# A two-block fp32 transformer kernel on one core: a rearranged hand-over between its stages, vector units moved within the down projections, keys before queries

## The chip, the core and the metric

The kernel runs on one core of a Trainium2 chip. The metric is the device time of one launch in microseconds, here the median of three runs. In all that follows PE is TensorE, DVE is VectorE, ACT is ScalarE, SP is the engine that issues nearly all DMAs, and an order of instructions is fixed for each engine by hand: the engines run ahead of one another as far as semaphores let them.

## What is computed

The reference takes x (256 tokens by 1024 features) through eight residual stages, all in fp32. Cut to what matters here:

```
x  = x + ga1 * mlstm(modulate(x))                      # stage "lstm"
x  = x + ga2 * conv_glu(modulate(x));  x = rmsnorm(x)  # stage "f0", then the final norm of block one
for each of the six sublayers f1, gla, f2, f3, mla, f4:
    h = rmsnorm(x, g_pre) * (1 + scale) + shift
    x = x + w * gate * rmsnorm(fn(h), g_post)          # fn: swiglu, gla_mixer, swiglu, swiglu, mla_mixer, swiglu
```

The shifts, scales and gates of the second block are products of silu(c) with conditioning matrices. swiglu is (silu(h Wg) * (h Wu)) Wd with a hidden width of 2816. mla_mixer makes a key and value latent of 256 from the output of f2, a query latent of 384 from its own input, normalises both, and multiplies them by key, value and query matrices.

## The kernel before, in words

**Products in three parts.** Each fp32 operand is split into a rounded part (type fp32r) and the rest. A product is three matmuls: rounded by rounded, rounded by rest, rest by rounded. The weights come as 219 chunks of 1 MB (`raw`), 128 x 2048 each. ACT rounds a chunk (`act_split`, line 223) and DVE takes the rest (`dve_split`, line 230). A raw slot is free again when the chunk five before it has been used (`s_pe`), so SP's issue of a chunk waits for PE.

**Vector units.** The conditioning product is done on DVE in 192 units of 0.5 MB: `dve_mod_unit` (line 675) multiplies 128 rows of 1024 weights with silu(c) and sums them. Two buffers (`mring`) hold the next two. SP issues a unit's transfer only behind the chunk that stands for it and only when the unit two before is done. The lists `UP_UNITS` and `DOWN_UNITS` say how many units DVE does after each split of a swiglu. `dve_ffn` does the split of down chunk d + 2, then `DOWN_UNITS[f][d]` units.

**The end of a stage.** A down or output projection of 8 or 22 feature tiles adds into four PSUM banks, one for each token tile t (of 128 tokens) and half h (of 512 columns). All chunks but the last run over all four banks. The last one or two run bank by bank (`pe_out_last`), so that bank (0,0) is complete first: with one chunk a bank takes 6 matmuls, with two it takes 12. Two chunks are used by f0 to f4, one by lstm, gla and mla.

**The seam.** `dve_boundary` and `act_boundary` then work for each token tile: ACT squares both halves of the rows of the output (line 493) and sums them, makes the mean of the first half plus epsilon (line 501, `uu`), and a logarithm and an exponential give the row's factor (lines 505, 506). DVE multiplies the output by the gate row (`dve_product`, line 597) and adds it to X (`dve_update`, line 606 or 610); ACT takes the norm of the new X the same way; DVE scales the rows (`dve_pre`, line 558, `XN`, two halves); PE transposes eight tiles (`pe_pre`, line 480); ACT applies shift and scale to each (`act_scaled`, line 545, one bank of four tiles at a time for t = 0); DVE rounds four tiles and takes the rest (`dve_pre_split`, lines 568 and 570), or one by one for t = 1 (lines 576, 580). After f0 a second norm of X (the final one of block one, line 617) stands between update and next norm. lstm and f0 have no norm of their output (`PLAIN`).

**The next stage's start.** Its first product (`pe_ffn`, `pe_gla`) takes all eight feature tiles of token tile 0. Before the last of them PE does the eight transposes of token tile 1, then goes through token tile 1. In f1 to f4 the transposes of token tile 0 stand before the last three matmuls of the stage before; behind lstm, f0, gla and mla they stand behind the last matmul.

**The latents.** `pe_kv` runs the key and value latent's two chunks with the transposes of token tile 1 between them, then the query latent: chunk DQ (4 half banks' worth) and, when chunk DQ_UQ has its rest, the last third of it; then the keys from the kv latent, the query latent's sum of squares, and the values.

## Time and profile before

| | us |
|---|---|
| median of 3 runs (1504.69 to 1509.45) | 1506.56 |
| the profiled execution's own time | 1504.5 |
| its span, first to last instruction | 1502.7 |
| PE busy | 1396.1 (93%) |
| DVE busy | 1132.1 (75%) |
| ACT busy | 800.9 (53%) |
| granted TensorE clock, mean | 0.973 |

Read it so: the span and the run's own time differ by 1.8 us that lie around the instructions. PE is busy for 1396.1 of 1502.7 us, so it is idle for 106.6; its busy time holds stretches in which the granted clock was 0.5 instead of 1.0. In the timeline a row merges like instructions of an engine: start, duration, engine, line, operation, and in brackets the idle time before and what ended it.

### The profile page before, as it was taken

How to read it: one execution, taken by the hardware profiler on the slowest of the kernel's cores; microseconds unless marked ns; L12 is line 12 of the kernel's file. 1: busy time of each engine (PE TensorE's matmuls, PEld its weight loads, DVE VectorE, ACT ScalarE, POOL GpSimd, SP SyncE). 2: the span in 40 equal slices, each digit the busy share in tenths (PEclk: the TensorE clock that was granted, in tenths of full speed). 3: DMA queues.
4: the chain of work that ended last, by engine and by line, in shares of the span. 5: the costliest groups of instructions: out<-in, count | busy, mean ns of one | idle time of the engine just before them, and what ended most of it. 6: DMA issues, size and time to landing. Idle time of an engine off the chain costs nothing.

```text
span 1502.7 us, 19113 instructions
## 1 busy us (share of the span) xinstructions
PE 1396.1 (93%) x7530; PEld 1195.5 (80%) x7530; DVE 1132.1 (75%) x1559; ACT 800.9 (53%) x1170; POOL 1.4 (0%) x6
## 2 busy tenths in 40 slices
PE   5989987899998999989989999989999896899997
PEld 4978876788876888878968888868887785688886
DVE  6787696699875988678677988679997764587653
ACT  6613534666636655365466555386554643665542
POOL 0000000000000000000000000000000000000000
PEclk9999998999999999999999999999999999999999
DMA  9576313477783887856544888849988530465551
GB/s 384 204 259 233 122 67 126 164 267 262 259 336 113 320 305 285 299 208 246 200 154 163 316 292 297 304 159 337 325 311 319 176 140 1 140 255 211 184 191 56
DMA packets 62713, 337.78 MB, mean 225 GB/s; under 512 B 6928, under 2 KB 9360, under 8 KB 34208
## 3 DMA queue, kind: packets, MB, share of 16 engines
q1 hardware_dynamic: 62160, 335.35, 61.6%
q8 instruction: 60, 0.98, 0.3%
q0 software_dynamic: 288, 1.05, 0.2%
q14 instruction: 29, 0.24, 0.1%
q10 hardware_dynamic: 176, 0.16, 0.0%
HBM read 335.49 MB, written 1.05 MB: 224 GB/s over the span
## 4 chain that ended last, share of the span: by engine, by line
PE 65%; DVE 17%; DMA 8%; ACT 7%; issue 3%; SPq 0%; ACTq 0%; DVEq 0%
PE bank L234 63%; DVE wlo L230 6%; DMA mring<-m_stream 6%; DVE mring L675 2%; DMA raw<-w_stream 2%; ACT T L545 1%; ACT whi L223 1%; ACT rstd L493 1%; ACT SGC L845 1%; DVE GU L885 1%; DVE T L907 1%; DVE rd L1338 1%; PE bank L480 1%; DVE SGC L896 1%; DVE SGC L893 1%
## 5 line engine op out<-in xcount | busy, mean ns | idle before, releaser
L234 PE MATMUL bank<-hh,whi 128*128 128x512 f32 (+1 forms) x2192 | 674.3, 368 | 16.0 <-DVE wlo L230 15.5
L230 DVE TENSOR_TENSOR wlo<-raw,whi 128x2048 fp32r<-128x2048 f32 x219 | 500.1, 2287 | 68.6 <-ACT whi L223 68.4
L234 PE MATMUL bank<-hh,wlo 128*128 128x256 f32 x1896 | 532.1, 281 | 0.0
L223 ACT ACTIVATE whi<-raw 128x2048 fp32r<-128x2048 f32 x219 | 418.0, 1913 | 160.7 <-PE bank L234 84.1
L234 PEld LDWEIGHTS bank<-hh,whi 128*128 128x128 f32 x2192 | 395.1, 190 | 93.9 <-DVE wlo L230 17.2
L234 PEld LDWEIGHTS bank<-hh,wlo 128*128 128x128 f32 x1896 | 360.2, 190 | 0.0
L675 DVE SCALAR_TENSOR_TENSOR mring<-mring,con 128x1024 f32<-128x1024 f32 x160 | 195.0, 1220 | 52.4 <-DMA mring<-m_stream 52.1
L234 PE MATMUL bank<-whi,hid_hi 128*128 128x512 f32 x440 | 173.7, 395 | 3.6 <-DVE wlo L230 3.6
L234 PE MATMUL bank<-whi,hh 128*128 128x512 f32 x480 | 163.1, 411 | 13.9 <-DVE hh L570 13.3
L234 PE MATMUL bank<-whi,hid_lo 128*128 128x512 f32 x440 | 172.6, 392 | 0.0
L234 PE MATMUL bank<-wlo,hid_hi 128*128 128x512 f32 x440 | 172.5, 392 | 0.0
L234 PEld LDWEIGHTS bank<-whi,hh 128*128 128x128 f32 x480 | 94.7, 197 | 39.9 <-issue 14.6
L837 ACT ACTIVATE GU<-bank 128x512 f32<-128x512 f32 x100 | 59.2, 592 | 100.6 <-PE bank L234 100.5
L234 PEld LDWEIGHTS bank<-whi,hid_hi 128*128 128x128 f32 x440 | 83.3, 189 | 21.4 <-DVE wlo L230 4.4
L234 PEld LDWEIGHTS bank<-whi,hid_lo 128*128 128x128 f32 x440 | 83.3, 189 | 17.7
L234 PE MATMUL bank<-wlo,hh 128*128 128x512 f32 x240 | 97.1, 405 | 0.0
L234 PEld LDWEIGHTS bank<-wlo,hid_hi 128*128 128x128 f32 x440 | 83.2, 189 | 16.8
L885 DVE TENSOR_TENSOR GU<-GU,bank 128x512 f32<-128x512 f32 x100 | 68.4, 684 | 33.4 <-ACT GU L837 33.3
L849 ACT ACTIVATE hid_hi<-T 128x256 fp32r<-128x256 f32 x110 | 46.0, 418 | 82.9 <-DVE T L907 82.9
L545 ACT ACTIVATE T<-bank,mod,coef 128x128 f32<-128x128 f32 x128 | 47.1, 475 | 26.8 <-PE bank L480 26.8
L907 DVE TENSOR_TENSOR T<-SGC,GU 128x256 f32<-128x256 f32 x100 | 42.3, 423 | 17.1 <-ACT SGC L845 15.0
L234 PEld LDWEIGHTS bank<-wlo,hh 128*128 128x128 f32 x240 | 47.4, 198 | 9.3
(290 smaller groups left out, 1267.1 us busy)
## 6 DMA issues: line engine op xcount, KB each, us to landing
raw<-w_stream SPq DMA_DIRECT2D x219, 1024.0 KB, 5.4
mring<-m_stream SPq DMA_DIRECT2D x192, 512.0 KB, 5.0
con<-const_d SPq DMA_DIRECT2D x1, 1472.0 KB, 10.8
XF<-xT SPq DMA_DIRECT2D x1, 1024.0 KB, 13.2
XC<-ctxT SPq DMA_DIRECT2D x1, 1024.0 KB, 12.5
y<-OUT SPq DMA_DIRECT2D x4, 256.0 KB, 2.9
cb<-c_row POOLq DMA_DIRECT2D x1, 512.0 KB, 7.4
con<-c_row POOLq DMA_DIRECT2D x1, 512.0 KB, 4.0
```

The lines of the kernel that those rows point to most:

```text
L223: nc.scalar.activation(w_hi(c, 0, CW), raw[:, c % RAW_SLOTS], ACT.Copy).then_inc(s_hi, 1)
L230: nc.vector.tensor_tensor(w_lo(c, 0, CW), raw[:, c % RAW_SLOTS], w_hi(c, 0, CW).bitcast(f32), ALU.subtract).then_inc(s_lo, 1)
L234: return nc.tensor.matmul(out, lhsT, rhs, start=start, stop=True, skip_group_check=True)
L480: nc.tensor.transpose(turned(t, j), XN[:, j * P:(j + 1) * P], ident).then_inc(s_tpn, 1)
L493: ins = nc.scalar.activation(junk, src(h), ACT.Square, accum_out=ss[:, n, h:h + 1])
L545: ins = nc.scalar.activation(TX[:, j], turned(t, j), ACT.Identity, bias=mod[:, m0 + j:m0 + j + 1], scale=coef[:, q, j:j + 1])
L675: nc.vector.scalar_tensor_tensor(out=mring[:, u % 2], in0=mring[:, u % 2], scalar=1.0, in1=(cb if u < COND_UNITS else cb2)[:], op0=ALU.mul ...
L837: nc.scalar.activation(GU[:, t % 2], banks[:, b:b + 2, SEQ:], ACT.Copy).then_inc(s_part, 1)
L845: nc.scalar.activation(SG[:, t % 3], gate, ACT.Silu).then_inc(s_silu, 1)
L849: nc.scalar.activation(hid_hi[:, t], T[:, t % 3], ACT.Copy).then_inc(s_hidhi, 1)
L885: nc.vector.tensor_tensor(GU[:, t % 2], GU[:, t % 2], banks[:, b:b + 2, 0:SEQ], ALU.add)\
L907: nc.vector.tensor_tensor(T[:, t % 3], SG[:, t % 3], value, ALU.mult).then_inc(s_prod, 1)
```

## The change

1. **Half means on DVE.** Line 501 leaves ACT (28 instructions); the new `dve_half` makes `uu` on DVE (28 instructions, each behind a new semaphore from ACT's first square), and ACT waits for it before the logarithm.
2. **First token tile in three pieces.** Of token tile 0, tiles 0, 1, 4, 5 go to bank 6 and are scaled on ACT, tiles 2, 3, 6, 7 go to bank 7 and are scaled on DVE (`dve_scaled`). DVE rounds them as tiles 0-1, 2-3 and 4-7, all three ahead of the update of token tile 1, and PE waits for a piece. The transposes come as two halves, and the second waits until tiles 0 to 3 have been scaled. The product of bank (1,0) moves ahead of `XN` of token tile 0, and ACT's square of it waits for that product.
3. **Units.** The units of a down projection are the same in number (14, and 12 in each of f1 to f3), but the last three splits have none before or between them but those of d = 7, and the coefficients are made one chunk sooner.
4. **Two chunks by token tile.** mla's last two chunks run bank by bank, as f0 to f4 do. lstm's and gla's run as chunk 2 for banks (0,0), (0,1), (1,0), chunk 3 for the same, then both for (1,1).
5. **Transposes** of token tile 0: half of them before the last three matmuls in f1, f2, f3 and now mla, the other half behind.
6. **Keys ahead of queries.** In `pe_kv` the keys come before the last third of the query latent, whose sum of squares moves into the values; DVE splits VALUES and DQ_UQ before the rotary key, and copies the keys before it builds `KRM`.

```diff
+        TAIL = [(i, n) for i in range(4) for n in range(2)]
+        HEAD_TAIL = [(0, 0), (1, 0), (2, 0), (0, 1), (1, 1), (2, 1), (3, 0), (3, 1)]
+        def pe_out_last(pe, c0, k0, hi, lo, order=TAIL, first=lambda: None, second=lambda: None, mid=None):
+            for i, n in order:
...
+                for g in range(2):
+                    if (i, n, g) == (3, 1, 1) and mid is not None:
+                        mid()
...
         def turned(t, j):
-            b, n = (j // 2, j % 2) if t else (6 + j // 4, j % 4)
+            b, n = (j // 2, j % 2) if t else (6 + j // 2 % 2, j // 4 * 2 + j % 2)
...
+        def pe_pre(pe, pre, t, halves=(0, 1)):
+            for half in halves:
+                pe.wait_ge(s_xn, 4 * PRES.index(pre) + 2 * t + half + 1)
+                for j in range(4 * half, 4 * half + 4):
+                    if t == 0 and j == 4:
+                        pe.wait_ge(s_t, MODULATED[pre] + 1)
+                    if t == 0 and j == 6:
+                        pe.wait_ge(s_vt, 2 * PRES.index(pre) + 1)
+                    nc.tensor.transpose(turned(t, j), XN[:, j * P:(j + 1) * P], ident).then_inc(s_tpn, 1)
...
+        def dve_half(dve, n):
+            if n in OTHERS:
+                dve.wait_ge(s_xsq, OTHERS.index(n) + 1)
+            else:
+                _, stage, t = ROW_NORMS[n]
+                dve.wait_ge(s_ysq, 4 * POSTS.index(stage) + 2 * t + 1)
+            nc.vector.tensor_scalar(uu[:, n:n + 1], ss[:, n, 0:1], 1.0 / D, EPS, ALU.mult, ALU.add).then_inc(s_uu, 1)
...
+        def dve_scaled(dve, name, tiles):
+            m0, _, q = PRE[name]
+            dve.wait_ge(s_tpn, turned_from(name) + bank_turned(0, tiles[-1]))
+            for j in tiles:
+                ins = nc.vector.tensor_scalar(TX[:, j], turned(0, j), coef[:, q, j:j + 1], mod[:, m0 + j:m0 + j + 1],
+                                              ALU.mult, ALU.add)
+            ins.then_inc(s_vt, 1)
...
         def dve_boundary(dve, stage):
             for t in range(2):
-                dve_product(dve, stage, t, 0)
...
+                if t == 0:
+                    dve_product(dve, stage, 0, 0)
+                elif pre:
+                    dve_scaled(dve, pre, (2, 3))
+                if stage not in PLAIN:
+                    dve_half(dve, rn("post", stage, t))
+                if t and pre:
+                    dve_first_piece(dve, pre, 0)
+                    dve_first_piece(dve, pre, 1)
+                dve_product(dve, stage, t, 1)
+                if t and pre:
+                    dve_scaled(dve, pre, (6, 7))
+                    dve_first_piece(dve, pre, 2)
                 dve_update(dve, stage, t)
                 if pre:
+                    dve_half(dve, rn("pre", pre, t))
+                if t == 0:
+                    dve_product(dve, stage, 1, 0)
...
-        DOWN_UNITS = [[2, 2, 1, 1, 2, 1, 2, 2, 1, 0, 0]] + [[1, 1, 1, 1, 1, 2, 1, 2, 2, 0, 0]] * 3 + [[0] * 11]
+        DOWN_UNITS = [[2, 2, 2, 2, 2, 2, 1, 1, 0, 0, 0]] + [[2, 1, 2, 1, 2, 1, 2, 1, 0, 0, 0]] * 3 + [[0] * 11]
...
-            after = {FT // 2 - 1: coefs}
+            after = {FT // 2 - 2: coefs}
...
             pe_pair(pe, DQ, 2)
-            pe.wait_ge(s_lo, DQ_UQ + 1)
-            for k in range(DT):
-                ins = mm3(bank[3][:, 0:SEQ], DQ_UQ, k, hhi[:, k], hlo[:, k], k == 0)
-            ins.then_inc(s_q2, 1)
+            pe.wait_ge(s_lo, KEYS + 1)
             pe.wait_ge(s_l, 2)
...
             ins.then_inc(s_pe, 1)
-            pe_stat(pe, N_QL)
+            pe.wait_ge(s_lo, DQ_UQ + 1)
+            for k in range(DT):
+                ins = mm3(bank[3][:, 0:SEQ], DQ_UQ, k, hhi[:, k], hlo[:, k], k == 0)
+            ins.then_inc(s_q2, 1)
             for n, (t, half, b) in enumerate(VALUE_BANKS):
+                if n == 2:
+                    pe_stat(pe, N_QL)
...
```

How the change moves DVE's instructions shows at three places. The first is the end of f1's down projection and the first half of the seam to gla. Line 675 (738 after) is a vector unit, 230 a weight split, 597 (653) the gate product, 610 (666) the update, 558 (613) the scaled rows. Before:

```order
L675 SCALAR_TENSOR_TENSOR mring,mod<-mring,con 128x1024 x2
L230 TENSOR_TENSOR wlo<-raw,whi 128x2048
L675 SCALAR_TENSOR_TENSOR mring,mod<-mring,con 128x1024 x2
L230 TENSOR_TENSOR wlo<-raw,whi 128x2048 x2
L687 TENSOR_TENSOR mod<-mod,cols 128x24
L691 SCALAR_TENSOR_TENSOR coef<-mod,cols 128x8
L597 TENSOR_TENSOR SGC<-bank,con 128x512 x2
L610 SCALAR_TENSOR_TENSOR X<-SGC,rr,X 128x512 x2
L558 TENSOR_SCALAR XN<-X,rr 128x512 x2
```

After:

```order
L738 SCALAR_TENSOR_TENSOR mring,mod<-mring,con 128x1024
L230 TENSOR_TENSOR wlo<-raw,whi 128x2048 x2
L750 TENSOR_TENSOR mod<-mod,cols 128x24
L754 SCALAR_TENSOR_TENSOR coef<-mod,cols 128x8
L230 TENSOR_TENSOR wlo<-raw,whi 128x2048
L653 TENSOR_TENSOR SGC<-bank,con 128x512
L518 TENSOR_SCALAR uu<-ss 128x1
L653 TENSOR_TENSOR SGC<-bank,con 128x512
L666 SCALAR_TENSOR_TENSOR X<-SGC,rr,X 128x512 x2
L518 TENSOR_SCALAR uu<-ss 128x1
L653 TENSOR_TENSOR SGC<-bank,con 128x512
L613 TENSOR_SCALAR XN<-X,rr 128x512 x2
```

No unit stands among the last three splits, and a third product stands before the scaled rows.

The second place is the same engine and seam from there to the scaled rows of token tile 1. Before:

```order
L597 TENSOR_TENSOR SGC<-bank,con 128x512
L568 CAST hh<-T 128x4x128
L570 TENSOR_TENSOR hh<-T,hh 128x4x128
L597 TENSOR_TENSOR SGC<-bank,con 128x512
L610 SCALAR_TENSOR_TENSOR X<-SGC,rr,X 128x512 x2
L568 CAST hh<-T 128x4x128
L570 TENSOR_TENSOR hh<-T,hh 128x4x128
L558 TENSOR_SCALAR XN<-X,rr 128x512 x2
```

After (588 is the new scaling of two tiles, 601 and 603 the rounding and the rest):

```order
L588 TENSOR_SCALAR T<-bank,coef,mod 128x128 x2
L518 TENSOR_SCALAR uu<-ss 128x1
L601 CAST hh<-T 128x2x128
L603 TENSOR_TENSOR hh<-T,hh 128x2x128
L601 CAST hh<-T 128x2x128
L603 TENSOR_TENSOR hh<-T,hh 128x2x128
L653 TENSOR_TENSOR SGC<-bank,con 128x512
L588 TENSOR_SCALAR T<-bank,coef,mod 128x128 x2
L601 CAST hh<-T 128x4x128
L603 TENSOR_TENSOR hh<-T,hh 128x4x128
L666 SCALAR_TENSOR_TENSOR X<-SGC,rr,X 128x512 x2
```

All of token tile 0 is now split before the update of token tile 1 begins.

The third place is DVE in the latents of mla, from the split of KEYS on (704, 767: a gate coefficient; 1798 to 1800, 1858 to 1860: the rotary key). Before:

```order
L704 SCALAR_TENSOR_TENSOR coef<-mod,cols 128x8
L1798 TENSOR_TENSOR KR<-bank,rd 128x256
L1799 TENSOR_TENSOR SGC<-bank,rd 128x256
L1800 TENSOR_TENSOR KR<-KR,SGC 128x256
L1798 TENSOR_TENSOR KR<-bank,rd 128x256
L1799 TENSOR_TENSOR SGC<-bank,rd 128x256
L1800 TENSOR_TENSOR KR<-KR,SGC 128x256
L230 TENSOR_TENSOR wlo<-raw,whi 128x2048 x2
L1900 MEMSET KRM 128x2048
```

After:

```order
L767 SCALAR_TENSOR_TENSOR coef<-mod,cols 128x8
L230 TENSOR_TENSOR wlo<-raw,whi 128x2048 x2
L1858 TENSOR_TENSOR KR<-bank,rd 128x256
L1859 TENSOR_TENSOR SGC<-bank,rd 128x256
L1860 TENSOR_TENSOR KR<-KR,SGC 128x256
```

The splits of VALUES and DQ_UQ stand in front of the rotary key.

## Rows read from the trace of the kernel before

**Rows 1.** Stretch in f1's down projection: length, busy us (PE, PEld, DVE, ACT, POOL), PEclk, DMA share, GB/s.

```profile
610.00:615.44 5.44, 5.44 (x26) 4.51 (x25) 2.85 (x3) 1.92 (x2) 0.00 (x0) 1.00 0.78 289
```

**Rows 2.** Timeline of PE: the transposes of token tile 0 at the seven seams.

```profile
252.35 1.10 PE L480 MATMUL bank<-con,XN 128*128 128x128 f32 x8 [1.66 <-DVE XN L558]
...
458.61 1.09 PE L480 MATMUL bank<-con,XN 128*128 128x128 f32 x8 [2.12 <-DVE XN L558]
...
654.94 1.09 PE L480 MATMUL bank<-con,XN 128*128 128x128 f32 x8 [2.85 <-DVE XN L558]
...
784.62 1.09 PE L480 MATMUL bank<-con,XN 128*128 128x128 f32 x8 [2.49 <-DVE XN L558]
...
980.57 1.97 PE L480 MATMUL bank<-con,XN 128*128 128x128 f32 x8 [3.05 <-DVE XN L558]
...
1175.05 1.96 PE L480 MATMUL bank<-con,XN 128*128 128x128 f32 x8 [3.01 <-DVE XN L558]
...
1300.55 1.21 PE L480 MATMUL bank<-con,XN 128*128 128x128 f32 x8 [2.50 <-DVE XN L558]
```

**Rows 3.** Timeline of PE: the transposes of token tile 1 at the same seams.

```profile
262.42 1.04 PE L480 MATMUL bank<-con,XN 128*128 128x128 f32 x8
...
469.80 1.03 PE L480 MATMUL bank<-con,XN 128*128 128x128 f32 x8
...
665.56 1.04 PE L480 MATMUL bank<-con,XN 128*128 128x128 f32 x8
...
795.23 1.03 PE L480 MATMUL bank<-con,XN 128*128 128x128 f32 x8
...
989.94 1.04 PE L480 MATMUL bank<-con,XN 128*128 128x128 f32 x8
...
1184.04 1.04 PE L480 MATMUL bank<-con,XN 128*128 128x128 f32 x8
...
1310.92 1.03 PE L480 MATMUL bank<-con,XN 128*128 128x128 f32 x8
```

**Rows 4.** Timeline of DVE at the seam from f1 to gla.

```profile
645.20 4.49 DVE L230 TENSOR_TENSOR wlo<-raw,whi 128x2048 fp32r<-128x2048 f32 x2
...
651.23 1.40 DVE L610 SCALAR_TENSOR_TENSOR X<-SGC,rr,X 128x512 f32<-128x512 f32 x2
654.40 0.88 DVE L558 TENSOR_SCALAR XN<-X,rr 128x512 f32<-128x512 f32 x2 [1.77 <-ACT rr L506]
```

**Rows 5.** Timeline of ACT at the same seam.

```profile
648.47 0.20 ACT L506 ACTIVATE rr<-rl 128x1 f32<-128x1 f32 x1
...
652.76 0.29 ACT L501 ACTIVATE uu<-ss,eps 128x1 f32<-128x1 f32 x1
...
655.72 1.50 ACT L545 ACTIVATE T<-bank,mod,coef 128x128 f32<-128x128 f32 x4 [0.45 <-PE bank L480]
```

**Rows 6.** Groups of DVE, shapes apart: times, then busy us and mean ns.

```profile
L570 DVE TENSOR_TENSOR hh<-T,hh 128x512 fp32r<-128x512 f32 x14 | 9.7, 692 | 0.5
...
L580 DVE TENSOR_TENSOR hh<-T,hh 128x128 fp32r<-128x128 f32 x56 | 15.4, 285 | 0.0
```

**Rows 7.** Three more stretches: behind a seam, in mla's latents, in f0's down projection.

```profile
656.30:663.10 6.80, 5.26 (x13) 3.61 (x12) 4.95 (x9) 5.58 (x18) 0.00 (x0) 0.50 0.45 154
1203.60:1209.20 5.60, 5.60 (x26) 5.60 (x27) 3.44 (x5) 0.08 (x1) 0.00 (x0) 0.50 0.00 0
418.00:424.00 6.00, 6.00 (x29) 4.95 (x28) 2.97 (x4) 3.59 (x2) 0.00 (x0) 1.00 1.00 388
```

**Rows 8.** Timeline of PE and of DVE in mla's latents.

```profile
1199.05 4.49 DVE L230 TENSOR_TENSOR wlo<-raw,whi 128x2048 fp32r<-128x2048 f32 x2
...
1203.59 0.80 PE L234 MATMUL bank<-hh,whi 128*128 128x256 f32 x2 [5.91 <-DVE wlo L230]
```

**Rows 9.** f0's down projection: PE before the last two chunks; the units' transfers.

```profile
443.71 0.50 PE L234 MATMUL bank<-whi,hid_hi 128*128 128x512 f32 x1 [2.57 <-DVE wlo L230]
...
DMA to landing us min/median/max: 3.5/5.4/7.0
```

More of the change, by code:

```diff
@@ L320, in pe_out_chunk @@
             ins.then_inc(s_pe, 1)
-        def pe_out_last(pe, chunks, k0, hi, lo, mid=None):
-            for i, (t, h) in enumerate(GROUPS):
-                for n, c in enumerate(chunks):
-                    for g in range(2):
-                        if i == 3 and n and g and mid is not None:
-                            mid()
-                        k = k0 + 2 * n + g
-                        ins = mm3w(out_bank(t, h), c, g * D + h * 512, tok(hi, k, t), tok(lo, k, t), False)
-                    if i == 3:
-                        ins.then_inc(s_pe, 1)
-                if i < 3:
+        TAIL = [(i, n) for i in range(4) for n in range(2)]
+        HEAD_TAIL = [(0, 0), (1, 0), (2, 0), (0, 1), (1, 1), (2, 1), (3, 0), (3, 1)]
+        def pe_out_last(pe, c0, k0, hi, lo, order=TAIL, first=lambda: None, second=lambda: None, mid=None):
+            for i, n in order:
+                t, h = GROUPS[i]
+                if (i, n) == (0, 0):
+                    first()
+                if (i, n) == (0, 1):
+                    second()
+                for g in range(2):
+                    if (i, n, g) == (3, 1, 1) and mid is not None:
+                        mid()
+                    k = k0 + 2 * n + g
+                    ins = mm3w(out_bank(t, h), c0 + n, g * D + h * 512, tok(hi, k, t), tok(lo, k, t), False)
+                if i == 3:
+                    ins.then_inc(s_pe, 1)
+                elif n:
                     ins.then_inc(s_yb, 1)
@@ L497, in act_row_rstd @@
                     act.wait_ge(s_ysq, ysq[0])
-                else:
-                    alink(act, ins)
-                if h == 0:
-                    alink(act, nc.scalar.activation(uu[:, n:n + 1], ss[:, n, 0:1], ACT.Identity, bias=eps[:, 0:1],
-                                                    scale=1.0 / D))
-                    if between is not None:
-                        between()
+                elif h:
+                    alink(act, ins)
+                else:
+                    ins.then_inc(s_xsq, 1)
+                    act.wait_ge(s_xsq, OTHERS.index(n) + 1)
+                if h == 0 and between is not None:
+                    between()
+            act.wait_ge(s_uu, n + 1)
             alink(act, nc.scalar.activation(rl[:, n:n + 1], ss[:, n, 1:2], ACT.Ln, bias=uu[:, n:n + 1], scale=1.0 / D))
@@ L525, in act_boundary @@
                     if t == 0 and stage in PLAIN:
-                        for b in range(2):
-                            act_scaled(act, pre, 0, b)
+                        act_scaled(act, pre, 0, (0, 1))
+                        act_scaled(act, pre, 0, (4, 5))
                 else:
@@ L532, in act_boundary, with act_scaled @@
             if pre:
-                act_scaled(act, pre, 1, None)
+                act_scaled(act, pre, 1, range(DT))
         def four(x):
             return x.rearrange("p (a b) -> p a b", a=4)
-        def act_scaled(act, name, t, b):
+        def act_scaled(act, name, t, tiles):
             m0, _, q = PRE[name]
             p0 = turned_from("f3" if name == "kv" else name)
-            act.wait_ge(s_h, U[name] + 2 * t)
-            for j in range(DT) if b is None else range(4 * b, 4 * b + 4):
+            act.wait_ge(s_h, U[name] + (2 if name == "kv" else len(PIECES)) * t)
+            for j in tiles:
                 act.wait_ge(s_tpn, p0 + bank_turned(t, j))
@@ L613, in dve_update @@
                 n = rn("fin", stage, t)
+                dve_half(dve, n)
                 dve.wait_ge(s_rr, n + 1)
@@ L1572, in pe_gla @@
             pe_gate_row(pe, "gla", (4, 5))
-            for j in range(2, 4):
-                out_chunk(j)
+            pe_out_last(pe, c + 15, 4, hhi, hlo, HEAD_TAIL, lambda: out_chunk(2), lambda: out_chunk(3))
             pe_pre(pe, "f2", 0)
@@ L1894, in dve_kv @@
             dve_gate_coef(dve, "mla")
+            dve_split(dve, VALUES)
+            dve_split(dve, DQ_UQ)
             dve.wait_ge(s_cs, 1)
@@ L1897, in dve_kv @@
             dve_rope(dve, KR[:, 0], KR[:, 1], *halves(5), s_kr)
-            dve_split(dve, VALUES)
-            dve_split(dve, DQ_UQ)
+            dve.wait_ge(s_pe, KEYS + 1)
+            for b in (0, 2):
+                nc.vector.tensor_copy(flat(KN[:, 2 * b:2 * b + 2]), bank[KEY_BANKS[b]][:]).then_inc(s_kn, 1)
             link(dve, nc.vector.memset(KRM[:], 0.0))
@@ L1904, in dve_kv @@
             ins.then_inc(s_kr, 1)
-            dve.wait_ge(s_pe, KEYS + 1)
-            for b in (0, 2):
-                nc.vector.tensor_copy(flat(KN[:, 2 * b:2 * b + 2]), bank[KEY_BANKS[b]][:]).then_inc(s_kn, 1)
             dve_latent(dve, 2, 3, N_QL, "g_q", (*halves(2), halves(3)[0]), qhi, qlo)
```

154 lines of the change are left out of this document (77 added, 77 removed).

## The prediction

> **What bounds the kernel now.** The page gives PE 93% of the span, so I looked for the rest in PE's idle time. Inside a stage there is none: in 5.44 us of a down projection PE is busy for all 5.44 (26 matmuls touch the stretch, 24 begin in it, one each 0.227) [rows 1]. The timeline has it at the seams: the transposes of token tile 0 wait for the scaled rows `XN`, 1.66 to 3.05 us at each of seven seams [rows 2]. I call P the start of the transposes of token tile 0 and P1 that of token tile 1. P1 is what a seam ends with: behind it PE always finds its next operands after about the same time, as everything there (scaling on ACT, rounding on DVE, the next weight split) hangs on these transposes. So a seam's gain is the shift of P1. From P to P1 it now takes 10.07, 11.19, 10.62, 10.61, 9.37, 8.99 and 10.37 us [rows 2, 3], for lstm to f0, f0 to f1, f1 to gla, gla to f2, f2 to f3, f3 to mla, and mla to f4. I call them A to G. In much of each such stretch TensorE runs at half rate: from 656.3 to 663.1 the granted clock is 0.50, the 1.2 GHz level [rows 7]. At E and F it has already fallen when the transposes come, which take 1.97 and 1.96 us there and 1.09 elsewhere, behind waits of 3.05 and 3.01 [rows 2].
>
> **Part one, P.** Take C. The product of bank (0,1) can follow at once when ACT has squared that bank, and the row's factor is there at 648.47 + 0.20 = 648.67 [rows 5]. But DVE is busy with two weight splits from 645.20 to 649.69 [rows 4], since it had done two vector units just before. Its update starts at 651.23. With no unit there, the splits are done as their chunks are rounded, and the update starts at about 648.8: 2.4 earlier. The mean `uu` stood on ACT between two squares, 0.29 [rows 5], 0.33 with its gap; DVE makes it while ACT squares the second half, so 0.33 goes once per norm of X. P moves by 2.7 at C. At E and F the same sum, from the same order of instructions, gives 2.9 each; at both the wait before P leaves about 0.1. At B the splits do not bind, since lstm and f0 need no norm of the output; two norms of X give 0.7. At A and D bank (0,1) is complete one bank's turn of 6 matmuls (6 x 0.227 = 1.36) sooner before the end of PE's work; with 0.33 that is 1.7, of which A can use 1.45 (its wait is 1.66 and 0.2 stays). At G it is complete two turns sooner: 2.7 + 0.33 = 3.1, which also the move of half the transposes ahead of three matmuls allows. Sum over A to G: 1.45 + 0.7 + 2.7 + 1.7 + 2.9 + 2.9 + 3.1 = 15.4 us. The product of bank (1,0), moved ahead of `XN`, costs 0.69 like row L570 [rows 6], and lies in the 1.77 that DVE waits for ACT before `XN` [rows 4]; without that cover it would cost up to 0.69 at each seam, 4.8 in all.
>
> **Part two, P to P1.** The new order fills DVE. From P: two tiles are transposed after 0.5; ACT scales two in 0.8 (four take 1.50 [rows 5]); DVE rounds tiles 0-1 and 2-3 in 0.75 each (a rest takes 0.285 for one tile and 0.692 for four [rows 6]; I take 0.42 for two, and 0.33 for the rounding); the product takes 0.6, the scaling of tiles 6-7 0.5, the third piece 1.1. The update can start at P + 5.0. From its start to `XN` it is 654.40 - 651.23 = 3.17 [rows 4], less 0.33, and 0.54 more to the transposes (654.94 - 654.40 [rows 2, 4]). So P1 = P + 8.4, whatever PE does: PE, which starts its matmuls at about P + 2.25, reaches the transposes at P + 7.4 and waits 1.0. At B a second norm and its product lie on that path, another 2.8: P1 = P + 11.2, and PE waits about 4 us there. The new scaling from PSUM on DVE has no row; for one tile it lies between the 0.285 of L580 and, if it were as slow as ACT, 0.47; I take 0.25 with overlap, the upper end adds 0.9 per seam. The differences to the present P1 - P are 1.7, 0, 2.2, 2.2, 1.0, 0.6, 2.0: 9.7 us.
>
> **The clock.** TensorE at half rate matters only where PE binds, which is behind P1. At B the new wait of 4 us ends there. Rows show the clock at 0.5 behind waits of 3.0 and 3.05 [rows 2], and a stretch of it lasts 5 to 7 us at C and in the latents [rows 7]; I take one of half that length, which costs 1.5. At the other six, waits come in pieces of at most 1.0 and I take 0.4 each, the part of such a loss that the wait before P1 does not absorb. Together -3.9.
>
> The Trainium skill, "TensorE: Matmul & The Clock Gate", part 1, says that idle time lets the chip gate TensorE to half rate, and that it needs sustained matmuls to come back; part 4 adds that transposes do not count as such. By that rule the wait at B, followed by transposes, is sure to cost what I charge, and the six others could pay the same. The trace agrees in that each seam's half-rate stretch takes in its transposes or what follows them.
>
> **Latents.** PE waits 5.91 us for DQ_UQ's rest [rows 8], which DVE makes from 1199.05 on, behind the rotary key. The keys' operands are there by then, so they run in that time. With the wait goes the half rate: from 1203.6 to 1209.2 PE was busy at a clock of 0.50 [rows 7], a loss of 2.8. But the query latent's norm now has less matmul work to hide behind: the query matrices wait for it and for the split of UQ1, which ACT starts only behind it. I estimate two new waits of 2.0 together, between 0 and 4.5 (two splits, as in [rows 4]). Gain 6.7.
>
> **Units.** In f1 to f3 the last two chunks no longer wait behind two units: f3 loses a wait of 1.0. In f0 PE waits 2.57 before the last two chunks [rows 9]. The new list puts two units to each of the first six chunks. A chunk of 1.05 MB and two units of 0.52 MB in a chunk's 5.44 us [rows 1] ask for 386 GB/s. In the fullest stretch the transfers moved 388 GB/s at a share of 1.00 [rows 7]: just enough, so the wait stays nearly whole, moved or not. I take 0.3; if each round of two units fell behind, up to 7 us are lost (rival 3's sum at the median landing), and if the wait went with its half rate, 4 are gained. The end of the kernel gains one `uu`, 0.3.
>
> The Trainium skill, "DMA: Bandwidth & Descriptors", section "Where 436 GB/s comes from", puts the limit from HBM at about 358 GB/s for a core. By it a chunk with two units would take 5.86 us instead of 5.44, and f0 would lose 2.5 in its first six chunks, so that the sum would be 2.5 less. The trace disagrees: 388 GB/s over 6 us.
>
> **Sum.** 15.4 + 9.7 + 6.7 + 1.0 + 0.3 + 0.3 - 3.9 = 29.5 us. The profiled execution took 1504.5; it becomes 1475.0. It lies 2.1 under the median of 1506.56, so the forecast against the median is **1477**.
>
> **The rivals.**
> 1. *Only the starts move.* The many small instructions on DVE and the new semaphores make P1 - P as long as it is now. For: DVE has no free time between P and P1 in my sum. Against: now much of it is PE at half rate. The gain loses 9.7: 1487. Chance 0.15.
> 2. *The seams close better.* The short waits never let the clock fall (3.9 more, even at B), and f0's wait goes with its half rate (2.3 + 1.7): 1469. For: the rows fall behind long waits. Against: B keeps 4 us. Chance 0.2.
> 3. *Units bunch, slower.* In the down projections a buffer of `mring` is refilled only when its unit is done, so two units cost at least a landing plus 1.23. With a mean landing L, f0's six rounds take 6(L + 1.23 - 5.44) too long, and each of f1 to f3 has 12 units, six rounds, in eight chunks: 6(L + 1.23) - 43.5 too long. The sum, 24L - 133.7, passes the gain of 29.5 at L = 6.8. For: landings reach 7.0 [rows 9], and SP issues the next chunk only behind these units. Against: the median is 5.4, at which f0 would lose 7 and the others nothing, and it was taken where transfers were fullest; part of a landing is time behind chunks that SP now issues later. At L = 7.5 the time is 1523. Chance 0.05.
> 4. *The change does not bite*, say because DVE's waits hold P where it is and f0 takes it all: within 0.3% of before. Chance 0.02.
>
> **How the numbers follow.** The forecast has 0.58. A measurement of this kernel can tell about 0.3%, 4.5 us, from no change. Faster: 0.58 + 0.15 + 0.2 = 0.93; same 0.02; slower 0.05. The range must leave out at most 0.2. Its low end is rival 2, 1469, less 1 for its bounds: 1468. Its high end takes in rival 1 at 1487, and the case that f0's loss of 7 and the product's 4.8 are both paid, 1477 + 7 + 4.8 = 1489: 1490.
>
> **What would show it.** Right: the waits before the transposes of token tile 0 are under 0.8 us but at B (1.4); P1 - P is 8.2 to 8.7, and 11 at B, with a wait of PE before it of 1.0 and 4.0; no wait of 5.9 in the latents, two short ones in the query matrices. Wrong: P1 - P above 9 at A, C, D, G; matmuls at half rate behind P1 at more seams than B; new waits for `wlo` in the first eight chunks of f0's down projection, with DVE waiting for `mring` before them.

## The result and the profile after

| | before | changed |
|---|---|---|
| median of the runs | 1508.01 us (1504.69 to 1510.21, 4 runs) | 1486.47 us (1484.04 to 1487.34, 4 runs) |
| profiled execution, its span | 1504.5, 1502.7 | 1486.22, 1484.3 |
| mean granted clock | 0.973 | 0.980 |

The ratio of changed to before is 0.9858, with a 95% interval of 0.9837 to 0.9879. In a second set of runs it was 0.9850 (0.9824 to 0.9876). The kernel is 1.4% faster, about 21.5 us. The forecast was 1477 (1468 to 1490) and a gain of 29.5, so the time is inside the range and faster, but a quarter of the expected gain is missing.

The stretches at half rate add up to 81.8 us within the span of the trace of before and to 58.1 in that of the changed kernel.

**The seams.** Timeline of PE in the changed kernel, the transposes at A, B, C and G (`L495` is now their line; token tile 0 goes in two halves). Columns are start, duration, engine, line, operation, tiles, count, and in brackets the wait before and what ended it. They answer to [rows 2, 3].

```profile
250.01 0.66 PE L495 MATMUL bank<-con,XN 128*128 128x128 f32 x4
258.55 1.10 PE L495 MATMUL bank<-con,XN 128*128 128x128 f32 x8 [0.86 <-DVE XN L613]
...
457.91 1.12 PE L495 MATMUL bank<-con,XN 128*128 128x128 f32 x4 [3.99 <-DVE XN L613]
469.72 1.11 PE L495 MATMUL bank<-con,XN 128*128 128x128 f32 x7 [2.69 <-DVE XN L613]
...
653.14 0.66 PE L495 MATMUL bank<-con,XN 128*128 128x128 f32 x4
661.76 0.98 PE L495 MATMUL bank<-con,XN 128*128 128x128 f32 x7 [0.91 <-DVE XN L613]
...
1285.38 0.66 PE L495 MATMUL bank<-con,XN 128*128 128x128 f32 x4
1294.01 1.09 PE L495 MATMUL bank<-con,XN 128*128 128x128 f32 x8 [0.92 <-DVE XN L613]
```

The waits before P of 2.85 and 2.50 at C and G [rows 2] are gone, and so are those at A, E and F; D keeps 0.81. P and P1 are, as in the prediction, the starts of the transposes of token tile 0 and 1. From P to P1 it takes 8.54, 8.62, 8.62, 8.63, 8.62 and 8.63 us at A, C, D, E, F and G, where it took 9 to 10.6. The odd one is B, with waits of 3.99 and 2.69.

The chain at C on DVE, which answers to [rows 4]:

```profile
644.93 2.29 DVE L230 TENSOR_TENSOR wlo<-raw,whi 128x2048 fp32r<-128x2048 f32 x1 [0.91 <-ACT whi L223]
...
649.74 1.41 DVE L666 SCALAR_TENSOR_TENSOR X<-SGC,rr,X 128x512 f32<-128x512 f32 x2
...
652.60 0.88 DVE L613 TENSOR_SCALAR XN<-X,rr 128x512 f32<-128x512 f32 x2 [0.55 <-ACT rr L538]
```

The last split now ends at 647.22 instead of 649.69. From update to `XN` it is 2.86, where it was 3.17.

**Clock and transfers.** Stretches of the changed kernel: length, busy us of PE, PEld, DVE, ACT and POOL, granted clock, DMA share, GB/s.

```profile
653.20:661.70 8.50, 7.24 (x32) 5.02 (x32) 6.64 (x18) 4.64 (x14) 0.00 (x0) 1.00 0.67 248
470.50:473.80 3.30, 3.30 (x10) 2.59 (x9) 2.64 (x15) 3.25 (x9) 0.00 (x0) 0.50 0.01 2
269.10:272.40 3.30, 3.30 (x12) 2.82 (x11) 1.67 (x1) 0.00 (x0) 0.00 (x0) 0.50 1.00 415
400.00:440.00 40.00, 38.87 (x180) 32.06 (x179) 30.25 (x32) 13.45 (x10) 0.00 (x0) 1.00 0.92 325
```

Seam C runs at full rate, where [rows 7] had 0.50. At C, D, E, F and G this trace has no half-rate stretch any more. One stands behind P1 of B (470.5), as forecast, and one at 269.1, at f0's third chunk, behind a wait of 2.36 for `wlo`. In the trace before, a drop came at 256.9, between P and P1 of A, where PE waited anyway, and none behind the wait of 2.41 for the same chunk. That the drop moved from there onto matmuls that set the pace is read from these places alone; the trace of e9 below has both. The last row is f0's down projection: 325 GB/s at a share of 0.92.

**New waits in down projections.** Timeline of PE in f0, f2, f3 and the latents:

```profile
435.72 0.50 PE L234 MATMUL bank<-whi,hid_hi 128*128 128x512 f32 x1 [1.13 <-DVE wlo L230]
442.71 0.50 PE L234 MATMUL bank<-whi,hid_hi 128*128 128x512 f32 x1 [1.25 <-DVE wlo L230]
...
960.97 0.50 PE L234 MATMUL bank<-whi,hid_hi 128*128 128x512 f32 x1 [0.98 <-DVE wlo L230]
...
1155.93 0.50 PE L234 MATMUL bank<-whi,hid_hi 128*128 128x512 f32 x1 [1.94 <-DVE wlo L230]
...
1206.47 0.39 PE L234 MATMUL bank<-qhi,whi 128*128 128x256 f32 x1 [0.58 <-DVE qlo L1850]
1210.05 0.39 PE L234 MATMUL bank<-qhi,whi 128*128 128x256 f32 x1 [1.16 <-DVE wlo L230]
```

The first two stand where [rows 9] had one of 2.57. The waits of f2 and f3 are there, where before had one of 1.01 (f3). The 5.91 of the latents [rows 8] is gone, with 0.58 and 1.16 in its place.

**What B waits for.** Timelines of ACT and DVE at the end of f0:

```profile
446.29 1.92 ACT L223 ACTIVATE whi<-raw 128x2048 fp32r<-128x2048 f32 x1 [3.64 <-DMA raw<-w_stream]
```

```profile
448.31 2.29 DVE L230 TENSOR_TENSOR wlo<-raw,whi 128x2048 fp32r<-128x2048 f32 x1 [3.04 <-ACT whi L223]
450.52 1.28 DVE L653 TENSOR_TENSOR SGC<-bank,con 128x512 f32<-128x512 f32 x2
```

A weight chunk lands late, its rounding and split follow, and only then does DVE get to the seam's first product. So in this trace the chain starts at a transfer, not at the order of instructions.

**Where the profiled 18.3 us came from.** The trace was cut at P and P1 of each seam; differences of changed less before, in us:

| piece | difference | piece | difference |
|---|---|---|---|
| start to P of A | -2.3 | D | -2.0 |
| A | -1.5 | f2 | -1.5 |
| f0 | +3.2 | E | -0.7 |
| B | +0.6 | f3 | +2.8 |
| f1 | -1.7 | F | -0.4 |
| C | -2.0 | mla | -7.9 |
| gla | -1.6 | G and f4 | -3.3 |

f0 and f3 became longer. Part of that is no effect of the change. In an up phase PE issues the same 640 matmuls with no gap, but at two paces. Stretches of 40 us in the up phases of f0 to f4, of the trace before; the first count in brackets is PE's matmuls:

```profile
330.00:370.00 40.00, 40.00 (x233) 35.24 (x232) 37.19 (x58) 26.55 (x36) 0.00 (x0) 1.00 0.69 252
510.00:550.00 40.00, 40.00 (x227) 34.67 (x227) 34.98 (x49) 21.89 (x29) 0.00 (x0) 1.00 0.85 298
840.00:880.00 40.00, 40.00 (x228) 34.67 (x227) 34.60 (x45) 22.29 (x29) 0.00 (x0) 1.00 0.81 292
1040.00:1080.00 40.00, 40.00 (x233) 34.98 (x232) 37.92 (x51) 24.05 (x30) 0.00 (x0) 1.00 0.92 329
1350.00:1390.00 40.00, 40.00 (x232) 34.95 (x231) 29.86 (x40) 22.60 (x30) 0.00 (x0) 1.00 0.61 218
```

The same for f0, f3 and f4 of the changed kernel:

```profile
330.00:370.00 40.00, 40.00 (x228) 34.72 (x227) 37.37 (x54) 27.41 (x36) 0.00 (x0) 1.00 0.74 264
...
1040.00:1080.00 40.00, 40.00 (x228) 34.68 (x227) 35.52 (x47) 21.87 (x28) 0.00 (x0) 1.00 0.90 319
1350.00:1390.00 40.00, 40.00 (x233) 34.99 (x232) 26.44 (x32) 22.53 (x31) 0.00 (x0) 1.00 0.55 197
```

A phase with 232 or 233 matmuls in 40 us is fast, one with 227 to 229 slow: 0.1733 against 0.1767 us from start to start, 2.1 us over 640. The profiled execution of before had three fast phases (f0, f3, f4), that of the changed kernel one (f4). Two phases are 4.2 us, so without this draw the pair would differ by 22.5, near the 21.5 of the medians. The shortfall against 29.5 is then 7 to 8 us.

### The profile page after: what moved, and what is told of

The parts are those of the page before. It is cut to its first block, busy times and chain, and to the rows that moved or that the text cites. A ratio compares the mean times of both kernels' runs of the same rounds, so it can differ in the third digit from the quotient of the medians.

```text
span 1484.3 us, 19174 instructions
## 1 busy us (share of the span) xinstructions
PE 1398.2 (94%) x7530; PEld 1191.1 (80%) x7530; DVE 1146.5 (77%) x1629; ACT 783.8 (53%) x1114; POOL 1.4 (0%) x6
## 4 chain that ended last, share of the span: by engine, by line
PE 63%; DVE 20%; ACT 7%; DMA 6%; issue 3%; SPq 0%; DVEq 0%; ACTq 0%
PE bank L234 61%; DVE wlo L230 6%; DMA mring<-m_stream 5%; DVE mring L738 3%; DMA raw<-w_stream 2%; ACT whi L223 1%; ACT rstd L524 1%; ACT T L578 1%; DVE GU L951 1%; ACT SGC L911 1%; DVE T L973 1%; DVE rd L1401 1%; PE bank L495 1%; DVE T L588 1%; DVE SGC L962 1%
## 5 line engine op out<-in xcount | busy, mean ns | idle before, releaser
L234 PE MATMUL bank<-whi,hh 128*128 128x512 f32 x480 | 159.4, 402 | 1.6 <-DVE hh L603 0.8
L234 PEld LDWEIGHTS bank<-whi,hh 128*128 128x128 f32 x480 | 91.5, 191 | 26.3 <-DVE hh L636 2.8
L937 DVE TENSOR_TENSOR hid_lo<-T,hid_hi 128x256 fp32r<-128x256 f32 x110 | 46.3, 421 | 2.9 <-ACT hid_hi L915 2.9
```

Of the source, the lines that this page charges most:

```text
L234: return nc.tensor.matmul(out, lhsT, rhs, start=start, stop=True, skip_group_check=True)
L937: nc.vector.tensor_tensor(hid_lo[:, t], T[:, t % 3], hid_hi[:, t].bitcast(f32), ALU.subtract).then_inc(s_hid, 1)
```

## The experiments

The theory behind them, **theory S**: the missing part is the units' transfers. In f0's down projection chunks and units fill the transfers, and in f2 and f3 two units per chunk make the next chunk late. The rivals are DVE's order and time, and an effect of the change on the pace of the up phases. Each kernel was timed four to six times beside 11 runs of before, whose median is given, and one of its executions was profiled. Medians of different sets compare best by their ratios to before.

**Units as before (e1_old_units).**

```diff
-DOWN_UNITS = [[2,2,2,2,2,2,1,1,0,0,0]] + [[2,1,2,1,2,1,2,1,0,0,0]] * 3 + [[0] * 11]
+DOWN_UNITS = [[2,2,1,1,2,1,2,2,1,0,0]] + [[1,1,1,1,1,2,1,2,2,0,0]] * 3 + [[0] * 11]
```

> The changed kernel, with the list of vector units per down chunk as before. Theory S (the stream sets the end of f0; elsewhere the two-unit rounds cost the waits of 0.98, 0.31 and 1.94 in f2 and f3): f0 keeps its end, since it moves the same 11 chunks and 14 units, so the wait before the transposes at seam B stays above 3 or turns back into one of about 2.5 in the down projection; the waits in f2's and f3's last chunks go (3.2 less, and 1.7 with the half-rate stretch at 1156), one of 1.0 in f3 comes back; the waits of 2.4 to 2.9 before the transposes at C, E and F come back (7.5 more). Together 3 to 5 us slower than the changed kernel. Rival U (the new list is what loses time in f0): seam B's transposes come 2 to 4 us earlier than in the changed kernel and the whole is within 1 us of it, or faster.

1488.99 (before 1508.09; ratio 0.9880, 0.9849 to 0.9910), 2.5 above the changed kernel's median, with overlapping intervals. The waits say more. Timeline of PE at B and C:

```profile
458.27 0.91 PE L495 MATMUL bank<-con,XN 128*128 128x128 f32 x4 [4.84 <-DVE XN L613]
...
657.61 1.12 PE L495 MATMUL bank<-con,XN 128*128 128x128 f32 x4 [3.06 <-DVE XN L613]
```

B keeps its wait with either list, so f0 is not lost by the new list, and rival U falls. The waits at C, E and F are back (3.06, 3.02, 3.81): the freed last chunks are what P gained there. The old list has waits for `wlo` of its own, 2.07 in f1 and 0.88 in f3, together as long as the 0.98 and 1.94 of the new list. What the new list is worth in all stays open: the profiled executions differ by 7.9 us, the medians by 2.5.

**Four units out of f0 (e2_f0_light).**

```diff
-DOWN_UNITS = [[2,2,2,2,2,2,1,1,0,0,0]] + ...
+DOWN_UNITS = [[2,1,2,1,2,1,1,0,0,0,0]] + ...
```

and one more unit at each of four places of `dve_lstm`, behind the splits of its chunks 6, 8, 9 and 11.

> The changed kernel, with four of the 14 vector units of f0's down projection made in the lstm stage instead, where DVE and the transfers have room. Theory S (f0's last chunks land late because chunks and units together fill the transfers): the waits of 1.13 and 1.25 in f0's down projection and all but 1.4 of the 3.99 before the transposes at seam B go, 4 to 5 us, and one half-rate stretch may go with them; 1482 or a little less against 1486.5. Rival D (the wait at B is the chain of two norms on DVE and ACT, whatever lands when): the waits in the down projection go, but B's transposes wait longer for it, and the time stays within 1 us of the changed kernel.

1486.91 (before 1508.09; ratio 0.9864, 0.9832 to 0.9896): no change in all, so the gain that was expected did not come. In f0 it did what theory S says: no wait in the down projection, 1.60 before P of B, and f0 took 193.96 instead of 199.36, with its up phase slow in both. But lstm grew by 8.75:

```profile
148.77 0.79 PE L234 MATMUL bank<-hh,whi 128*128 128x256 f32 x2 [5.54 <-DVE V L1360]
```

Ahead of it DVE stands 2.50 for a unit's landing (at 140.14) and then makes two more units, while PE needs the values that DVE must read out. My "room in lstm" was a mean of busy time; the place was on the path.

**The key and value stage as before (e3_kv_old).** The order of `pe_kv`, `act_kv` and `dve_kv` was set back to that of before.

> The changed kernel, with the order of the key and value stage as before (query latent ahead of the keys, rotary key ahead of its splits). If my term for the latents holds: the wait of about 5.9 before the query latent's last third comes back with its half rate, the two waits of 0.58 and 1.16 go, and the kernel is 6.5 us slower than the changed one (5.5 to 8). Rival: the seams alone had already shortened it (the weights have more lead), and it is 3 or less.

1492.39 (before 1508.09; ratio 0.9904, 0.9877 to 0.9930), 5.9 above the changed kernel. From P1 of F to P of G it took 114.61 instead of 108.61, with the old wait in its old length:

```profile
1196.31 0.80 PE L234 MATMUL bank<-hh,whi 128*128 128x256 f32 x2 [5.91 <-DVE wlo L230]
```

The term of 6.7 measures 6.0.

**The half mean on ACT again (e4_uu_act).**

```diff
 def dve_half(dve, n):
+    return
...
-    act.wait_ge(s_uu, n + 1)
+    if h == 0:
+        alink(act, nc.scalar.activation(uu[:, n:n+1], ss[:, n, 0:1], ACT.Identity,
+                                        bias=eps[:, 0:1], scale=1.0 / D))
```

> The changed kernel, with each half mean square on ACT again, between the two squares, instead of on DVE. My sum charged 0.33 us for each norm of X on the path: two at a seam, four at B, one at the end, 17 in all, 5.6 us slower. Rival: DVE is full between the first transposes of token tile 0 and those of tile 1, so its small instruction costs there what it saves on ACT, and only the norm of token tile 0 gains: 7 to 8 norms, 2.5 us slower.

1489.98 (before 1508.09; ratio 0.9877, 0.9846 to 0.9907), 3.5 above. By pieces: 8.87 to 8.96 from P to P1 at the six plain seams instead of 8.54 to 8.63, 12.47 instead of 11.81 at B, a wait before P that is longer by 0.32 or 0.33 at A, C, E, F and G and by 0.68 at D (two norms), and 0.33 at the end: 5.3 in all. So 0.33 a norm holds wherever the chain binds, the stretch to P1 included, where the rival had it free. The medians show 3.5 of it.

**The changed kernel again (e5_again).**

> The changed kernel once more, unaltered. In the traces so far the matmuls of an up phase run at one of two paces, 0.1737 or 0.1767 us from start to start over the same 640 instructions. Theory E (the pace is drawn anew in each execution, and is no effect of the change): at least one up phase stands at the other pace than in the first profile of the changed kernel (slow, slow, slow, slow, fast for f0 to f4), and the single times spread over 5 us or more. Rival C (the change set it): the same five paces, and times within 3 us.

1484.61 (1481.27 to 1490.49, 6 runs; before 1506.02; ratio 0.9850, 0.9824 to 0.9876). Stretch in f4's up phase:

```profile
1350.00:1390.00 40.00, 40.00 (x229) 34.68 (x228) 26.15 (x32) 21.90 (x29) 0.00 (x0) 1.00 0.54 188
```

It is slow where the first profile had 233, and f4 took 192.62 instead of 190.26. The pace is drawn per execution: theory E. The wait in f3's last chunks was 2.96 instead of 1.94, so these waits differ between executions too, and no half-rate stretch stands behind P1 of B.

**Small units (e6_small_units).** In the down projections, each unit loads 64 of its 1024 columns and its product is zero, so these modulation values are left out of the result.

```diff
-sp.dma_start(mring[:, u % 2], m_stream[u])
+n = 64 if u in down_units else D
+sp.dma_start(mring[:, u % 2, 0:n], m_stream[u][:, 0:n])
```

> The changed kernel, but the vector units of the down projections load 64 of their 1024 columns, and their products are multiplied by zero, with the same instructions on every engine: those modulation columns are left out. Theory S (transfers bind the end of f0, and make the waits of f2 and f3): no wait for wlo over 0.5 in any down projection, 1.4 to 1.6 before the transposes at seam B, f0 shorter by 4 to 5 us, f2 by 1, f3 by 2 to 3.5: together 7 to 10 us faster than the changed kernel, less than 1480. Rival D (DVE's time for two units a chunk holds back the splits): the same waits as before, within 1 us.

1475.51 (before 1506.02; ratio 0.9788, 0.9766 to 0.9811), 9.1 less than e5's 1484.61 beside the same runs of before. Timeline of PE at B, and the same 40 us as above:

```profile
452.81 0.66 PE L495 MATMUL bank<-con,XN 128*128 128x128 f32 x4 [1.47 <-DVE XN L613]
```

```profile
400.00:440.00 40.00, 40.00 (x186) 33.29 (x185) 35.24 (x37) 15.38 (x11) 0.00 (x0) 1.00 0.63 215
```

All waits of the down projections are gone with the same instructions on DVE, and P of B waits 1.47, against the 1.4 of my sum. The median landing of a chunk in f0's down projection (issues from 400 to 450) falls from 7.7 to 4.9 us. Rival D falls. f0 took 193.86 instead of 199.36, f2 182.50 instead of 183.81, and f3 182.88 instead of 187.90, all at the slow pace: the transfers of the units cost f3 nearly as much as f0. What this does not separate is the rate of the transfers from the time of one landing with two buffers, since both went down.

**The start of f0 (e7_f0_start).**

```diff
-act.wait_ge(s_c2, 16)
-nc.scalar.activation(cb2, cb2, ACT.Silu).then_inc(s_cb, 1)
 act_swiglu(act, 0)
...
 def rows(t):
+    if f == 0 and t == 2:
+        act.wait_ge(s_c2, 16)
+        nc.scalar.activation(cb2, cb2, ACT.Silu).then_inc(s_cb, 1)
...
+if f == 0:
+    act_split(act, c0 + 4)
 for t in range(FT):
```

and DVE splits that chunk with the two before it.

> The changed kernel, with two moves at the start of f0: the Silu of the second conditioning row, with its table, stands behind the third tile of the up phase instead of ahead of the rounding of two chunks, and the fifth chunk is rounded and split before the first tile instead of behind the second. If the waits of 2.36 at 266 and 3.21 at 282 are ACT's order alone, both go (under 0.3 each), with two half-rate stretches of 3.4 behind them: 5.5 + 2 x 1.7 = 8.9 us. Rival S2 (f0's end hangs on the stream, whose end doesn't move): the gain is given back at the waits of the down projection and of seam B, and 3 us or less are left.

1482.66 (before 1506.02; ratio 0.9832, 0.9807 to 0.9858), 2 less than e5, with overlapping intervals, so as a whole the gain isn't shown. The profiled execution, 1476.00, was the fastest of the six. In it the wait of 2.36 and its half rate went; the 3.21 became

```profile
285.46 0.50 PE L234 MATMUL bank<-hh,whi 128*128 128x512 f32 x1 [1.71 <-DVE wlo L230]
292.60 0.50 PE L234 MATMUL bank<-hh,whi 128*128 128x512 f32 x1 [1.32 <-DVE wlo L230]
```

since DVE now makes units ahead of the split that PE wants. f0 took 192.40 instead of 199.36, 2.1 of it by a fast up phase, so 4.9. The expectation of 8.9 failed: ACT's order was not the only cause of the second wait. The profile has more than the rival's 3 us left in f0; the medians, with 2, can't tell the two apart. The waits of its down projection (1.51, 1.62, and 3.10 before P) stayed. By the order of the program, chunks are issued as PE frees slots, so an earlier start of the down projection moves the stream along with it; no run separates this.

**Spread lists (e8_lists).** The kernel before, and

```diff
-UP_UNITS = [[0,1,1,2] + [1,0,1] * 6, ...
+UP_UNITS = [[0,1,1,2] + [1,1,1,1,0,1] * 3, ...
-DOWN_UNITS = [[2,2,2,2,2,2,1,1,0,0,0]] + [[2,1,2,1,2,1,2,1,0,0,0]] * 3 + ...
+DOWN_UNITS = [[2,1,1,2,1,1,2,1,0,0,0]] + [[2,1,1,2,1,2,1,1,1,0,0]] * 3 + ...
```

> The kernel before this one (both moves at f0's start), with the units spread: three of f0's 14 down units made in zero slots of its up phase, the others as 2, 1, 1, 2, 1, 1, 2, 1, and 2, 1, 1, 2, 1, 2, 1, 1, 1 in f1 to f3. Theory S: f0 is 4 us shorter than with the list of the changed kernel, since 3 units of 0.52 MB fewer cross the full stretch, f2 and f3 wait 1 to 2 us less. Rival D: DVE is 0.93 busy in f0's up phase, the added units bring waits there, and nothing is won.

1474.41 (before 1506.02; ratio 0.9779, 0.9756 to 0.9801), 8.3 less than e7. f0 took 189.15 with a slow up phase, 5.4 less than e7 at equal pace; P of B waits 1.48. f2 and f3 had no wait for `wlo`. One unit with the ninth chunk cost a wait before P of F, 2.18. The added units brought no wait to f0's up phase.

**The output products chunk by chunk (e9_tail_by_chunk).** From the changed kernel, for lstm, gla and mla (whose call is given this order too):

```diff
-HEAD_TAIL = [(0,0), (1,0), (2,0), (0,1), (1,1), (2,1), (3,0), (3,1)]
+HEAD_TAIL = [(0,0), (1,0), (2,0), (3,0), (0,1), (1,1), (2,1), (3,1)]
```

> The changed kernel, but the last two chunks of the down products of lstm, gla and mla run chunk by chunk, as before, with only the last one bank by bank. If my sum for the heads of A, D and G holds: the transposes of token tile 0 come 1.2 to 1.4 us later at A and D and 2.4 to 2.8 later at G, the stretches from there to those of token tile 1 stay at 8.6, and the wait before P is 2.2, 2.2 and about 2.5; 5 to 5.5 us in all. Rival: at the seams another wait ends last (the splits, or ACT), and A, D and G together lose less than 2.

1492.41 (before 1507.03; ratio 0.9904, 0.9885 to 0.9922), 6 to 8 above the changed kernel's two medians. Timeline of PE at D and G:

```profile
783.30 0.95 PE L495 MATMUL bank<-con,XN 128*128 128x128 f32 x4 [2.16 <-DVE XN L613]
...
1289.40 1.12 PE L495 MATMUL bank<-con,XN 128*128 128x128 f32 x4 [2.84 <-DVE XN L613]
```

P of D came 1.37 later, as expected, and A waits 1.32 before P. At G the wait grew by 2.7, from 0.13 to 2.84, within the 2.4 to 2.8 expected; that mla took 4.3 longer is no measure of it, since the other traces that have this mla give it 106.67 to 110.28. Not expected either: P to P1 grew as well, to 9.59 and 9.29. Behind waits of this length the granted clock is at half rate:

```profile
784.00:790.70 6.70, 6.06 (x18) 4.56 (x17) 5.88 (x15) 3.60 (x11) 0.00 (x0) 0.53 0.20 84
1289.50:1296.00 6.50, 6.50 (x21) 5.34 (x22) 5.48 (x15) 2.83 (x9) 0.00 (x0) 0.54 0.44 159
```

So at D and G an earlier P was worth more than its own shift: the stretch to P1 was 0.97 and 0.66 shorter without the wait, at the 2.4 GHz level.

**Other lists (e10_lists2).** From e8: f0's up phase begins 0, 0, 1, 2, 2; f1 to f3 have 2, 1, 2, 1, 1, 2, 1, 2, 0, 0, 0.

> The fastest kernel so far (e8_lists), with two changes of its lists: no unit with f0's second tile and two with its fifth instead, and none behind the ninth down chunk of f1 to f3. Theory: the waits of 1.50 and 1.31 at f0's start (DVE makes units ahead of a split that PE waits for) shrink by 1.2 each at most, and the 2.18 before the transposes of seam F goes below 0.3: 2 to 4 us less than e8_lists. Rival: DVE has no free time in f0's up phase any more, and the waits move behind the fifth tile; the gain is the 2 at F alone.

1475.18 (before 1507.03; ratio 0.9784, 0.9765 to 0.9804): nothing over e8. The waits at f0's start stayed (1.50, 1.31), a third of 1.04 came behind the fifth tile, and P of F waits for nothing, but f2 waits 1.14 and f3 2.61 for `wlo`. The same twelve units in eight chunks cost a wait of PE; in nine they cost the seam's P. In these two traces the second is smaller; the medians don't tell them apart.

**The last piece behind the update, at B only (e11_f0_seam).** From e8; `between` scales, rounds and splits tiles 4 to 7, and is taken out ahead of the update:

```diff
 if stage == "f0":
     dve_half(dve, n)
+    between()
     dve.wait_ge(s_rr, n + 1)
```

> e8_lists, and in f0's seam alone the scaling and rounding of tiles 4 to 7 stand behind the update, in the time in which DVE waits for the final norm's factor. Theory (at B the chain of two norms from DVE's update binds the second transposes, and DVE idles in it): P to P1 at B shrinks from 11.4 by 1.3 to 1.8, with the wait before P1 from 2.7 to about 1. Rival: PE waits for the third piece in its place, and P to P1 shrinks by 0.3 or less.

1469.40 (before 1507.03; ratio 0.9745, 0.9725 to 0.9765). P to P1 at B is 10.14 instead of 11.40, a little under the expected 1.3, and PE waits 0.92 before P1:

```profile
447.56 0.66 PE L495 MATMUL bank<-con,XN 128*128 128x128 f32 x4 [2.24 <-DVE XN L613]
...
457.70 1.09 PE L495 MATMUL bank<-con,XN 128*128 128x128 f32 x8 [0.92 <-DVE XN L613]
```

The half-rate stretch behind P1 of B, there in e8 at 460, is gone too. This is the fastest kernel of the study, 15 to 17 us under the changed kernel's two medians. Against e8 the ratios give about 5 us, more than the 1.3 at B, and their intervals overlap.

**Both (e12_both).** The lists of e10 with the seam of e11.

> Both of the kernels before together. If their gains are in separate places they add up: 1.5 us less than e10_lists2, 2 to 4 less than e11_f0_seam.

1475.22 (before 1507.03; ratio 0.9773, 0.9751 to 0.9794), the expectation failed. B is at 10.14 again, but e10's lists bring waits for `wlo` of 1.24, 1.90 and 3.13 in f1, f2 and f3. They show no gain over e8's lists, with or without the new seam.

## Why the prediction was right or wrong

- **Part one, P: right.** At C, E, F and G nothing over 0.2 is left before P, at D 0.81. e1 puts the freed last chunks at waits of 3.06, 3.02 and 3.81, where I had 2.4 for them alone; e9 puts the new turn at D at 1.37, where I had 1.36. At B the wait is 3.99 instead of 1.4, for the reason under Units.
- **Part two, P to P1: the mechanism right, the gain 2 us smaller.** 8.54 to 8.63 against 8.4, with a wait of 0.7 to 0.9 before P1 against 1.0; at B 11.4 to 11.8 against 11.2, with a wait of 2.69 against 4. Over the seven seams that is 7.7 us gained against 9.7. Rival 1 did not happen. The scaling from PSUM on DVE, 0.404 a tile, was nearer to the upper bound of 0.47 than to the 0.25 taken; a pair takes 0.72.
- **Half means: right in size.** 0.33 a norm, 5.3 us in all by e4's pieces, 3.5 by its median.
- **Clock: mis-sized.** I charged 2.4 for six seams; in the changed kernel's two traces none has a half-rate stretch from P to P1. In e1, e3 and e12 seam D has one, and P to P1 is only 0.04 to 0.13 longer there: the wait before P1 takes up the rest. B's came in one of the two traces (3.4 long, 1.7 lost). One at 269 costs 1.7, which I had not seen.
- **Latents: right.** 6.0 by e3 against 6.7; the new waits are 1.74 against 2.0.
- **Units: the step that failed.** "386 GB/s ... the transfers moved 388 GB/s ...: just enough, so the wait stays nearly whole", and a gain of 1.0 in f3. I read the rate from six full microseconds. Over 24 us of f0's down projection the transfers moved 355 GB/s before and 337 in the changed kernel, at shares of 0.95 and 0.94:

```profile
408.00:432.00 24.00, 24.00 (x110) 19.91 (x108) 18.74 (x18) 8.64 (x6) 0.00 (x0) 1.00 0.95 355
```

```profile
408.00:432.00 24.00, 24.00 (x108) 19.84 (x107) 16.53 (x18) 8.65 (x6) 0.00 (x0) 1.00 0.94 337
```

  At 337 a chunk and two units (2.10 MB) take 6.2 us, not 5.44. So what seam A won was lost at B, whose P waits 3.99 instead of 1.4; f2 got a wait of 0.98, and f3, instead of losing its wait of 1.0, waits 1.85 to 3.74 in the seven traces with this list, at times with a half-rate stretch. That is near rival 3's mechanism, at a smaller size. e6 shows the cause: with most of the units' transfers taken out, the gain over before is 30.5 us.
- **The rule of the page.** The Trainium skill, "DMA: Bandwidth & Descriptors", section "Where 436 GB/s comes from", has about 358 GB/s from HBM for one core. I set it aside for a row of 6 us. The 24 us above lie near it, 355 and 337, but the trace does not bear it out as a limit. Of the trace of before:

```profile
4.00:44.00 40.00, 26.06 (x106) 21.06 (x107) 24.57 (x17) 27.37 (x28) 0.66 (x1) 0.89 1.01 419
```

  At the kernel's start, with chunks and inputs to move and no unit yet, 40 us run at 419 GB/s. So 358 is no limit of this core's transfers, and the lower rate in f0 goes with its mix of chunks and units. From 408 to 432 of the changed kernel's trace a packet of a unit (4096 bytes) took 196 ns on the mean and one of a chunk (8192 bytes) 336, where one of 8192 bytes took 311 from 4 to 44: a unit's byte costs a sixth more than a chunk's beside it. Whether the size of the packets does that, no run tests. By the page's figure the sum would have been 2.5 less, nearer to the result, though still too high.

The forecast's terms, laid on the pieces of the two traces (f0 and f3 with 2.1 taken off for the pace), in us:

| piece | forecast | measured |
|---|---|---|
| start to P of A | -1.5 | -2.3 |
| P to P1, seven seams | -9.7 | -7.7 |
| f0 | -0.6 | +1.1 |
| f1 | -1.2 | -1.7 |
| gla and f2 | -3.8 | -3.2 |
| f3 | -3.5 | +0.7 |
| mla | -9.4 | -7.9 |
| f4 | +0.1 | -1.5 |

Summed up: of what is missing, the largest part is f3 (4.2) and f0 with its seam B (2.3), where e6 puts the cause with the units' transfers. P to P1 at the other six seams (1.3) and mla (1.5) fell short too, and three pieces gave more than I had for them, f4 most: the half-rate stretch at the kernel's end is 3.5 long instead of 6.7. The time fell inside the range partly since these make up for some of the loss. The runs do not divide it finer, since the waits in f1 to f3 change from execution to execution.

## What to carry to other kernels

Read a sustained rate of transfers over a stretch as long as the work that needs it, and with the same mix of transfers; a full share over a few microseconds does not tell whether a schedule that needs that rate for 40 can hold it. Work that is moved away from a seam's chain has to go where both its engine and its transfer have room: four units in a stage that looked idle by its mean cost 8.75 us, nearly twice their own 4.9 on DVE, and twelve units in nine chunks left PE shorter waits than twelve in eight, though the medians of e8 and e10 are the same. Fill an engine's wait with work that is needed later (e11), and cut kernels at fixed instructions into pieces before comparing two profiles.
